# Attention probabilities times the value columns alone, in two column groups, with the softmax sums added on GpSimd and finished by a product with ones

## The chip, the cores and the metric

The kernel runs on one NeuronCore of a Trainium2 chip. The metric is the device time in microseconds (us) of one execution. Before the change it was measured three times: 1147.48 us in the median, from 1145.49 to 1149.68.

## What is computed

Two layers of a diffusion trunk over 256 context tokens and 512 latent tokens, model width 1024, all in float32. Each layer projects the normalised tokens, runs three mixers side by side (gated linear attention "GLA", six heads of latent attention "MLA", six query heads of grouped attention "GQA" on two key/value heads), gates them and multiplies by an output matrix. The change is in the softmax attention of the twelve MLA and GQA heads:

```python
def attend(q, keys, vals, scale):
    s = jnp.einsum('bqhgd,bkhd->bhgqk', q, keys) * scale
    p = jax.nn.softmax(s.astype(jnp.float32), axis=-1).astype(vals.dtype)
    return jnp.einsum('bhgqk,bkhe->bqhge', p, vals)
# latent queries (512) attend to context and latent keys (768); context queries (256) to context keys
y = latent_attention(q, k, v, kc, vc, scale) * silu(z)
yc = attend(qc, kc, vc, scale) * silu(zc) if l < DEPTH - 1 else None
```

Value vectors have 64 columns in both kinds of heads. Layer 1 needs no context outputs.

## The kernel before, in words

Five engine programs are written by hand and meet through semaphores: `up(stage, step)` marks a step as done, `at(stage, step)` is the value another engine waits for. Each engine works strictly in the order in which its program is written. SP issues all weight blocks `W`, two buffers in turn, when TensorE has finished the block before last. Of PSUM's eight banks six form a ring: `open_` (L1238) takes the next one for each group of products and waits until the group six places before was released with `let_go`; the two `pv` banks hold the attention outputs, in turn.

**Scores and exponentials.** Scores are made transposed, a tile of 128 keys by all queries of a block, so that the exponential needs no transpose before it meets the values. A head is one block of 512 latent queries over six key tiles, and in layer 0 a block of 256 context queries over two key tiles before it. The "units" of a head are these tiles: j = 0 to 7 in layer 0, 0 to 5 in layer 1. The negated maximum of each query is found first (`maxes` L1444 on TensorE, `maxima` L1110 on VectorE, `max_rows` L1460 on TensorE, `neg_max` L741 on ScalarE) and comes in as an extra row of the queries against a row of ones of the keys (97 rows), so ScalarE's one instruction, L771, makes exp(score - max) from PSUM into one of four buffers `prob`. MLA scores are one float32 product (L1548), GQA scores two products of rounded parts (L1552, L1554).

**Values and sums.** `pv` (L1482) multiplies a probability tile by a stationary operand of 128 columns: 64 columns of values and 64 of ones, which lie beside one another in `vm` (MLA, 192 columns for a pair of heads: values, ones, values) and `vg` (GQA, the same shape). For even heads it takes columns 0 to 127, for odd ones 64 to 191. So one half of the `pv` bank gets the unnormalised output and the other half 64 equal copies of the softmax sum. A float32 product is recorded as two matmul records of the same shape. `recip` (L705, ScalarE: Ln, L712, and Exp with scale -1, L714) turns the sums into reciprocals `rd`, and `normalise` (L1136, VectorE: L1145, L1150) multiplies the output by them and by the gate in `Y`.

**The order around it on TensorE** (L1522 to L1569). For each head h: project the queries of head h+1 (`project_q`, L1425), one pending value product, the max rows of head h (L1466), project the keys of h+1 (`project_k`, L1435), the other pending value product; then for each unit the scores, the value products of all but the last two units (`flush(2)`), and from unit `MAX_FROM` on (3 in layer 0, 2 in layer 1) two maximum products of head h+1 (L1457). The projections exist for MLA heads alone, so at the boundaries into heads 5 to 11 only value products and max rows stand. In layer 0 heads 1 to 4, and heads 7 and 8 of both layers, also carry a modulation block: `mod` (L1273) multiplies eight tiles of weights in four column groups of 32, and `mod_turn` (L1284, L1290) turns the rows. The GLA output (`gla_o`, L1394) writes two 64-column products into the two halves of a bank (L1399).

**GpSimd** (L366 to L492): rounds the keys of each MLA head (`round_k`, L384), fills `vm`'s ones (L437), fills the padding rows of the GQA keys and queries (`k_pad`, L459 and L460; `q_pad`, L464, which `maxes` of heads 6 and up wait for), subtracts the rounded output weights from the weights (`w_lo`, L471, sixteen instructions a layer, needed by the out products L1579 to L1581), issues the DMAs that bring the residual back (`x_back`, L478 and L482). It makes the block masks of GLA's states too (L430).

**ScalarE** (L756 to L811) has for each head: copies of the next head's queries and keys (`head_in`, `gqa_in`), the exponentials, `recip` of the head before behind exponential 0 and of the context block behind exponential 3, `round_q`, in the last two heads sixteen `w_high` roundings (L733), and at the end of the layer `y_high` (L738).

## Time and profile before

| | |
|---|---|
| three timed runs, median (range) | 1147.48 us (1145.49 to 1149.68) |
| profiled execution, first to last instruction | 1146.1 us |
| mean granted TensorE clock | 0.974 of full |
| TensorE matmul busy | 1072.0 us, 94% |
| weight loads | 610.6 us, 53% |
| VectorE, ScalarE, GpSimd busy | 440.2, 368.3, 127.5 us |
| instructions | 11426 |
| layer 0 attention, MLA and GQA heads | 362 to 584 us of the span |
| layer 1 attention | 945 to 1088 us |

The profiled execution's own time is known as its span, 1146.1 us; the device time that is measured without a profile has its median 1.4 us above it. A busy share counts an engine's instructions, not its waits. Matmul records overlap in a stream, since a record's length holds the array's latency: a 512-wide float32 record is 0.59 us long while the next one starts 0.43 us behind it. The chain of waits, which follows the work that ended last, therefore counts such a record with 0.43 us. Granted clock 1.00 is 2.4 GHz, 0.5 is 1.2 GHz.

### The profile page before, as it was taken

The page shows a single profiled execution, that of the slowest core. Times are in us where ns is not written, and L with a number is a line of the kernel's source. Part 1 is how long each engine was busy: PE and PEld are TensorE (multiplying, and loading weights), DVE is VectorE, ACT ScalarE, POOL GpSimd, SP SyncE. Part 2 cuts the span into 40 slices and gives each one's busy share as a digit, 9 for nine tenths or more (in the row PEclk, how much of TensorE's full clock was granted, in tenths as well). Part 3 has the DMA queues.
Part 4 walks back from the last instruction along what each step waited for, and adds up shares of the span by engine and source line. Part 5 has one row for each costly group of instructions (what it writes and reads, how often), then busy time and mean ns, then how long its engine had stood idle before and what let it go on. Part 6 is the DMA issues. An engine that isn't in the chain of part 4 may idle for free.

```text
span 1146.1 us, 11426 instructions
## 1 busy us (share of the span) xinstructions
PE 1072.0 (94%) x4139; PEld 610.6 (53%) x4139; DVE 440.2 (38%) x797; ACT 368.3 (32%) x690; POOL 127.5 (11%) x148
## 2 busy tenths in 40 slices
PE   2799999999999999999899899999998999999996
PEld 0455555655455544455568655555444544445474
DVE  1342103312473433554453433122237444454453
ACT  3322113100113344566650332112001234455712
POOL 2000000000242001000440200000003300100530
PEclk8899999999999999999999899999998899999998
DMA  9801012201200222122022411120222000003021
GB/s 351 288 1 56 2 54 74 74 19 56 74 1 1 74 74 77 71 74 74 1 111 69 145 51 55 55 73 1 74 75 73 1 1 1 0 29 119 1 93 73
DMA packets 50965, 74.29 MB, mean 65 GB/s; under 512 B 7812, under 2 KB 30688, under 8 KB 50784
## 3 DMA queue, kind: packets, MB, share of 16 engines
q1 hardware_dynamic: 47088, 60.81, 15.8%
q0 software_dynamic: 3824, 12.77, 3.0%
q8 instruction: 35, 0.57, 0.2%
q14 instruction: 18, 0.15, 0.0%
HBM read 69.37 MB, written 4.19 MB: 64 GB/s over the span
## 4 chain that ended last, share of the span: by engine, by line
PE 86%; DVE 4%; issue 3%; ACT 3%; DMA 2%; POOL 1%; SPq 1%; ACTq 0%; POOLq 0%; DVEq 0%
PE bank L1329 30%; PE pv L1497 10%; PE bank L1548 6%; PE bank L1320 5%; PE bank L1457 3%; PE bank L1579 3%; PE bank L1581 3%; PE bank L1580 3%; PE bank L1435 3%; PE bank L1466 3%; PE bank L1425 2%; DMA W<-in_w_mod 2%; PE bank L1273 2%; PE bank L1405 2%; PE bank L1474 2%
## 5 line engine op out<-in xcount | busy, mean ns | idle before, releaser
L1329 PE MATMUL bank<-hA,W 128*128 128x512 f32 (+1 forms) x992 | 348.3, 510 | 2.7 <-DVE hA L882 1.5
L1329 PEld LDWEIGHTS bank<-hA,W 128*128 128x128 f32 x992 | 187.8, 190 | 154.3 <-issue 142.4
L771 ACT ACTIVATE hA<-bank 128x512 f32<-128x512 f32 (+1 forms) x168 | 93.1, 563 | 91.9 <-PE bank L1548 64.0
L1127 DVE TENSOR_REDUCE mxp<-bank 128x1 f32<-128x384 f32 x192 | 96.5, 551 | 51.0 <-PE bank L1457 50.8
L1497 PE MATMUL pv<-hA,vg 128*128 128x512 f32 (+1 forms) x168 | 85.1, 588 | 6.7 <-ACT hA L771 6.4
L1497 PE MATMUL pv<-hA,XA 128*128 128x512 f32 (+1 forms) x168 | 82.1, 570 | 1.5 <-ACT hA L771 1.5
L1548 PE MATMUL bank<-hA 97*128 97x512 f32 (+1 forms) x168 | 78.1, 565 | 0.0
L1145 DVE SCALAR_TENSOR_TENSOR hA<-pv,hA 64x512 f32<-64x512 f32 (+1 forms) x36 | 21.6, 600 | 113.5 <-ACT hA L714 113.3
L1320 PE MATMUL bank<-W,hA 128*128 128x384 f32 x192 | 63.7, 486 | 0.0
L1580 PE MATMUL bank<-W_parts,hA_parts 128*128 128x512 f32 x160 | 62.3, 389 | 0.0
L911 DVE SCALAR_TENSOR_TENSOR YA<-tz,bank 128x512 f32<-128x512 f32 (+1 forms) x24 | 14.4, 599 | 108.3 <-ACT tz L573 108.3
L573 ACT ACTIVATE tz<-bank 128x512 f32<-128x512 f32 (+1 forms) x24 | 12.6, 527 | 134.1 <-PE bank L1329 134.1
L412 POOL MEMSET hA<- 128x2048 f32 x2 | 3.6, 1807 | 447.1 <-PE bank L1329 447.1
L1497 PEld LDWEIGHTS pv<-hA,XA 128*128 128x128 f32 x168 | 30.3, 189 | 40.4 <-issue 37.3
L1320 PEld LDWEIGHTS bank<-W,hA 128*128 128x128 f32 x192 | 36.5, 190 | 26.5 <-issue 3.8
L1457 PE MATMUL bank<-rounded 96*128 96x384 f32 (+1 forms) x108 | 45.3, 505 | 2.6 <-DVE nmx L1119 1.6
L536 ACT ACTIVATE tz<-XA 128x1024 f32<-128x1024 f32 x16 | 16.9, 1054 | 91.3 <-DVE XA L1229 88.8
L520 ACT ACTIVATE rs<-bank,eps 128x512 f32<-128x512 f32 (+1 forms) x20 | 12.0, 602 | 96.2 <-PE bank L1348 57.6
L1497 PEld LDWEIGHTS pv<-hA,vg 128*128 128x128 f32 x168 | 29.0, 191 | 25.5 <-ACT hA L771 12.7
L1224 DVE TENSOR_TENSOR rt<-bank,cqkv 128x512 f32<-128x512 f32 x20 | 13.8, 692 | 67.4 <-PE bank L1581 53.6
L1548 PEld LDWEIGHTS bank<-hA 97*128 97x128 f32 x168 | 30.4, 189 | 16.3 <-issue 15.0
L1273 PE MATMUL bank<-W,sc 128*32 128x512 f32 x192 | 29.3, 738 | 9.6 <-DMA W<-in_w_mod 8.7
(209 smaller groups left out, 1467.9 us busy)
## 6 DMA issues: line engine op xcount, KB each, us to landing
W<-in_w_mod SPq DMA_DIRECT2D x12, 2048.0 KB, 8.0
W<-in_w_in SPq DMA_DIRECT2D x6, 1536.0 KB, 8.5
W<-in_w_in SPq DMA_DIRECT2D x8, 1024.0 KB, 6.1
W<-in_w_out SPq DMA_DIRECT2D x4, 2048.0 KB, 7.8
W<-in_w_in SPq DMA_DIRECT2D x8, 512.0 KB, 4.3
XA<-in_x SPq DMA_DIRECT2D x4, 512.0 KB, 10.9
XA<-in_x POOLq DMA_DIRECT2D x4, 512.0 KB, 7.4
x_between_layers<-XA POOLq DMA_DIRECT2D x4, 512.0 KB, 2.9
```

Of the source, the lines that this page charges most:

```text
L771: act.activation(prob[slot % 4][:, 0:nq], ps("sc", l, h, q0, kt)[:, 0:nq], ACT.Exp, scale=MLA_SCALE if h < MLA_H else GQA_SCALE)\
L1127: dve.tensor_reduce(mxp[:, t, half:half + 1], ps("mx", l, h, q0, t, half)[:, 0:384], AX, ALU.max).then_inc(*up("part_max", l, h, q0, t, half))
L1273: mm = pe.matmul(p[32 * j:32 * j + 32, :], sc[:, k, :], W[:, i % 2, k, :], start=(r == 0), stop=(r == 1), skip_group_check=True)
L1320: mm = pe.matmul(p[:, 0:384], hT[:, k, t * P:(t + 1) * P], w[:, k, 0:384], start=(k == 0), stop=(k == KD - 1))
L1329: mm = pe.matmul(p[:, 0:c[1]], w[:, k, s * P:s * P + P], hT[:, k, c[0]:sum(c)], start=(k == 0), stop=(k == KD - 1))
L1435: mm = pe.matmul(p[0:64, 0:c[1]], wukv[:, f, h, 0:64], cqkv[:, 2 + f, c[0]:sum(c)], start=(f == 0), stop=(f == 1))
L1457: close(pe.matmul(p[:, 0:n], q[:, t * P:t * P + P], k[:, n * half:n * half + n], start=True, stop=True), "mx", l, h, q0, t, half)
L1466: mm = pe.matmul(p[96:97, P * j:P * j + P], nmx[:, h % 2, t:t + 1], ident, start=True, stop=True)
L1497: mm = pe.matmul(pv_banks[i % 2][:, 0:nq], v, prob[sl % 4][:, 0:nq], start=(kt == 0), stop=(kt == nkt - 1))
L1548: mm = pe.matmul(p[:, 0:nq], kh[h % 2][0:97, keys], qh[h % 2][0:97, queries], start=True, stop=True)
L1579: pe.matmul(p[:], hi, w_hi[n][k], start=(k == 0), stop=False)
L1580: pe.matmul(p[:], hi, w_lo[:, i % 2, k, :], start=False, stop=False)
```

## The change

The value tiles lose their ones: `vm` and `vg` hold 64 columns for each head. Each value product becomes two, with the same 64 value columns stationary: the first half of the queries goes to partitions 0 to 63 of the `pv` bank, the second half to partitions 64 to 127. The sums are made elsewhere: GpSimd adds a block's probability tiles as they come (`prob_sums`, one add a tile from the second on) into one of two buffers `psum`, and TensorE multiplies that total by 64 columns of ones, in the same two halves (`den`), behind the scores of unit 0 of the next head (latent block) or behind unit 3 (context block). `den` takes a bank of the ring. ScalarE's reciprocal reads that bank: 128 partitions by half the queries. `normalise` scales in two instructions. The probability buffers are six instead of four, and the exponential waits for the buffer's add as well as its product. On GpSimd the whole order of the attention part is rewritten into one loop over heads.

```diff
+PROBS = 6
-        prob = [hA[:, 3072 + 512 * i:3584 + 512 * i] for i in range(4)]
-        rd, un = hA[:, 5120:5632], hA[:, 5632:6144]
+        rd, un = hA[:, 5120:5376], hA[:, 5632:6144]
-        vm = XA[:, 0:3456].rearrange("p (t r c) -> p t r c", t=TILES, r=3)
+        vm = XA[:, 0:2304].rearrange("p (t h v) -> p t h v", t=TILES, h=MLA_H)
-        vg = sb("vg", [P, TILES, 2, 192])
+        vg = sb("vg", [P, TILES, 2, 64])
+        more = sb("more", [P, 4, 512])
+        prob = [hA[:, 3072 + 512 * i:3584 + 512 * i] for i in range(4)] + [more[:, i, :] for i in range(2)]
+        psum = [more[:, 2 + i, :] for i in range(2)]
...
GpSimd:
-                pool.memset(vm[:, :, :, 64:128], 1.0).then_inc(*up("vm_ones", l))
...
-                for h in heads[1:MLA_H]:
-                    round_k(l, h)
...
+                def prob_sums(h, q0, nq, nk):
+                    i = pv_index(l, h, q0)
+                    total = psum[i % 2][:, 0:nq]
+                    first = slot_of(l, h, q0)
+                    if i >= 2:
+                        pool.wait_ge(*at("filled", "den", *pv_owner(i - 2)))
+                    pool.wait_ge(*at("prob", l, first + 1))
+                    pool.tensor_tensor(total, prob[first % PROBS][:, 0:nq], prob[(first + 1) % PROBS][:, 0:nq],
+                                       ALU.add).then_inc(*up("prob_sum", l, first + 1))
+                    for sl in range(first + 2, first + nk // P):
+                        pool.wait_ge(*at("prob", l, sl))
+                        pool.wait_ge(*at("prob_sum", l, sl - 1))
+                        pool.tensor_tensor(total, total, prob[sl % PROBS][:, 0:nq], ALU.add)\
+                            .then_inc(*up("prob_sum", l, sl))
+                    pool.wait_ge(*at("prob_sum", l, first + nk // P - 1))
...
+                for h in heads:
+                    if len(qbs(l)) == 2:
+                        prob_sums(h, *qbs(l)[0])
+                    if h + 1 < MLA_H:
+                        round_k(l, h + 1)
+                    if h == MLA_H - 1:
...
+                            pool.memset(k_low[g][64:96, :].bitcast(F32), 0.0).then_inc(*up("k_pad", l, g, 0))
+                            pool.memset(k_low[g][96:97, :].bitcast(F32), 1.0).then_inc(*up("k_pad", l, g, 1))
+                    if h in (MLA_H - 1, MLA_H):
+                        b = h - MLA_H + 1
+                        pool.wait_ge(*at("filled", "sc", l, MLA_H + b - 2, 256, TILES - 1))
+                        pool.wait_ge(*at("k_pad", l, 1, 1))
+                        pool.memset(q_high[b][64:96, :].bitcast(F32), 0.0).then_inc(*up("q_pad", l, b))
+                    if h == MLA_H + 1:
...
+                                pool.dma_start(X[:, t, :], src).then_inc(*dma("x_back", l))
...
+                    prob_sums(h, *qbs(l)[-1])
+                    if h == heads[-2]:
+                        weights_low(0, range(4))
...
+                weights_low(0, range(4, KD))
+                weights_low(1, range(KD))
...
ScalarE, recip:
+                    n2 = nq // 2
+                    act.wait_ge(*at("filled", "den", l, h, q0))
+                    act.activation(rd[:, 0:n2], ps("den", l, h, q0)[:, 0:n2], ACT.Ln).then_inc(*up("den_ln", l, h, q0))
+                    let_go(("den", l, h, q0), "den_ln", l, h, q0)
+                    act.activation(rd[:, 0:n2], rd[:, 0:n2], ACT.Exp, scale=-1.0).then_inc(*up("recip", l, h, q0))
...
ScalarE, exponentials:
-                        if slot >= 4:
-                            act.wait_ge(*at(*prob_reader(l, slot - 4)))
+                        if slot >= PROBS:
+                            act.wait_ge(*at(*prob_reader(l, slot - PROBS)))
+                            act.wait_ge(*at("prob_sum", l, summed(l, slot - PROBS)))
...
VectorE, normalise:
+                    for e in range(2):
+                        half = slice(64 * e, 64 * e + 64)
+                        dve.scalar_tensor_tensor(out=un[r:r + 64, n2 * e:n2 * e + n2], in0=pv[half, 0:n2], scalar=0.5,
+                                                 in1=rd[half, 0:n2], op0=ALU.mult, op1=ALU.mult)\
+                            .then_inc(*up("o_scaled", l, h, q0))
...
TensorE:
-                    mm = pe.matmul(pv_banks[i % 2][:, 0:nq], v, prob[sl % 4][:, 0:nq], start=(kt == 0),
-                                   stop=(kt == nkt - 1))
+                    v = vm[:, kt, h, :] if h < MLA_H else vg[:, kt, (h - MLA_H) // 3, :]
+                    for e in range(2):
+                        mm = pe.matmul(pv_banks[i % 2][64 * e:64 * e + 64, 0:n2], v,
+                                       prob[sl % PROBS][:, n2 * e:n2 * e + n2], start=(kt == 0), stop=(kt == nkt - 1))
...
+                def den(h, q0, nq, nk):
+                    p, n2 = open_("den", l, h, q0), nq // 2
+                    total = psum[pv_index(l, h, q0) % 2]
+                    pe.wait_ge(*at("prob_sum", l, slot_of(l, h, q0) + nk // P - 1))
+                    for e in range(2):
+                        mm = pe.matmul(p[64 * e:64 * e + 64, 0:n2], ones[:, 0:64], total[:, n2 * e:n2 * e + n2],
+                                       start=True, stop=True)
+                    close(mm, "den", l, h, q0)
...
                         flush(2)
+                        if j == 0 and h:
+                            den(h - 1, *qbs(l)[-1])
+                        if j == 3 and len(qbs(l)) == 2:
+                            den(h, *qbs(l)[0])
                         if j >= MAX_FROM[l]:
                             maxes(groups[:2])
...
                 flush(0)
+                den(heads[-1], *qbs(l)[-1])
```

The copies of values become one instruction a tile on VectorE (`mla_v`, and the GQA part of "tok") instead of two.

## Rows read from the trace of the kernel before

**Rows 1.** The page, part 1: busy time and share of the span of each engine.
```profile
PE 1072.0 (94%) x4139; PEld 610.6 (53%) x4139; DVE 440.2 (38%) x797; ACT 368.3 (32%) x690; POOL 127.5 (11%) x148
```

**Rows 2.** Windows: window, length, busy us (instructions), TensorE's clock, DMA.
```profile
490.00:584.00 94.00, 85.33 (x341) 48.62 (x340) 48.23 (x90) 64.01 (x119) 21.34 (x17) 0.98 0.13 45
```

**Rows 3.** Chain of waits in layer 1's MLA heads: start us, us, what.
```profile
954.60 0.35 PE bank L1457 x2
954.95 0.86 PE bank L1548 x2
955.81 0.86 PE pv L1497 x2
...
962.63 2.73 PE bank L1435 x8
965.36 1.05 PE pv L1497 x2
```

**Rows 4.** Groups of TensorE by shape: count, busy us, mean ns, idle before.
```profile
L1497 PE MATMUL pv<-hA,vg 128*128 128x512 f32 x144 | 77.2, 618 | 3.3 <-ACT hA L771 3.0
...
L1497 PE MATMUL pv<-hA,vg 128*128 128x256 f32 x24 | 7.9, 409 | 3.5 <-ACT hA L771 3.4
```

**Rows 5.** Timeline of TensorE, layer 0, head 6: start us, us, what [idle before].
```profile
493.22 0.70 PE L1497 MATMUL pv<-hA,vg 128*128 128x256 f32 x2 [1.18 <-ACT hA L771]
```

**Rows 6.** Timeline of TensorE, layer 1, a boundary between GQA heads.
```profile
1064.10 1.03 PE L1466 MATMUL bank<-con,nmx 128*1 128x128 f32 x8 [0.27 <-DVE nmx L1131]
```

**Rows 7.** Timeline of TensorE, the GLA output of layer 0.
```profile
341.95 0.65 PE L1399 MATMUL bank<-hA,XA 128*64 128x256 f32 x4 [0.43 <-POOL hA L430]
342.53 0.82 PE L1405 MATMUL bank<-glav,hA 128*128 128x64 f32 x3
```

**Rows 8.** Chain of waits around a modulation block of layer 0.
```profile
384.39 1.85 PE bank L1273 x16
386.24 1.06 PE bank L1548 x2
```

**Rows 9.** Groups of ScalarE by shape: the reciprocal's two instructions.
```profile
L714 ACT ACTIVATE hA<-hA 64x512 f32<-64x512 f32 x24 | 15.1, 629 | 0.8
L712 ACT ACTIVATE hA<-pv 64x512 f32<-64x512 f32 x24 | 14.2, 592 | 0.7
...
L714 ACT ACTIVATE hA<-hA 64x256 f32<-64x256 f32 x12 | 5.0, 415 | 0.4
...
L712 ACT ACTIVATE hA<-pv 64x256 f32<-64x256 f32 x12 | 4.5, 379 | 0.3
```

**Rows 10.** Two lines of GpSimd: count, duration ns min/median/max.
```profile
L430 POOL TENSOR_TENSOR hA<-XA,con x20: 1028/1170/1515, 306.6 to 893.0; 128x512 f32<-128x512 f32 x20
...
L471 POOL TENSOR_TENSOR W_parts<-W,gqk_parts x12: 1255/1270/1450, 559.6 to 1077.9; 128x512 fp32r<-128x512 f32 x12
...
L471 POOL TENSOR_TENSOR W_parts<-W,sq_parts x4: 1482/1738/1987, 580.5 to 1094.0; 128x512 fp32r<-128x512 f32 x4
```

**Rows 11.** Timelines, layer 0, heads 4 and 5: GpSimd, ScalarE, TensorE.
```profile
454.44 0.73 POOL L459 MEMSET wuq_parts<- 32x768 f32 x1
...
456.80 0.73 POOL L460 MEMSET wukv_parts<- 1x768 f32 x1
...
476.52 0.38 ACT L771 ACTIVATE hA<-bank 128x256 f32<-128x256 f32 x1
...
477.37 0.59 PE L1457 MATMUL bank<-wuq_parts,hA_parts 96*128 96x256 f32 x2
```

**Rows 12.** Timeline of TensorE in head 10 of layer 0; the window behind it.
```profile
562.84 0.74 PE L1457 MATMUL bank<-wukv_parts,hA_parts 96*128 96x384 f32 x2 [2.10 <-DVE nmx L1119]
...
563.00:567.00 4.00, 4.00 (x11) 2.67 (x11) 2.90 (x7) 2.93 (x6) 4.00 (x4) 0.69 0.02 4
```

**Rows 13.** Timelines at the end of layer 0's attention: ScalarE, TensorE.
```profile
582.13 1.06 ACT L771 ACTIVATE hA<-bank 128x512 f32<-128x512 f32 x2
...
584.17 0.80 PE L1579 MATMUL bank<-gqk_parts,hA_parts 128*128 128x512 f32 x1
```

More of the change, by code:

```diff
@@ L304, in pv_owner, with slot_of, summed @@
             return (0, i // 2, (0, 256)[i % 2]) if i < 24 else (1, i - 24, 256)
+        def slot_of(l, h, q0):
+            return h * sum(nk // P for _, _, nk in qbs(l)) + (2 if q0 and l < DEPTH - 1 else 0)
+        def summed(l, slot):
+            per = sum(nk // P for _, _, nk in qbs(l))
+            u = slot % per
+            return slot + 1 if u == 0 or (l < DEPTH - 1 and u == 2) else slot
         def prob_reader(l, slot):
@@ L370, in _ @@
             pool.memset(keep[:], 1.0).then_inc(*up("pool_init", "keep1"))
-            pool.memset(vg[:, :, :, 64:128], 1.0).then_inc(*up("pool_init"))
             pool.memset(wa[:], 0.0).then_inc(*up("pool_init", "wa"))
@@ L450, in _, with weights_low @@
                             .then_inc(*dma("brow_in", l))
[L451 to L467 removed]
+                def prob_sums(h, q0, nq, nk):
[13 more added lines that the diff above has]
+                    pool.wait_ge(*at("prob_sum", l, first + nk // P - 1))
+                def weights_low(n, ks):
                     i = W_POS[("out", l, n)]
[L469 removed]
+                    for k in ks:
                         pool.wait_ge(*at("w_hi", l, n, k))
@@ L920, in _ @@
                             src = ps("tok", l, t)[:, 256:384].rearrange("p (g v) -> p g v", g=2)
-                            for half in range(2):
-                                dve.tensor_copy(vg[:, t, :, 128 * half:128 * half + 64], src)\
-                                    .then_inc(*up("vg", l, t, half))
-                            let_go(("tok", l, t), "vg", l, t, 1)
+                            dve.tensor_copy(vg[:, t, :, :], src).then_inc(*up("vg", l, t))
+                            let_go(("tok", l, t), "vg", l, t)
                     elif item == "ga":
```

77 lines of the change are left out of this document (29 added, 48 removed).

## The prediction

> **What bounds the kernel now.** I read the page's busy shares, then the stages in a table of windows, then the chain of waits inside the attention stages, and last the timelines of single heads. The page: TensorE is busy for 94% of the span, VectorE for 38%, ScalarE for 32%, GpSimd for 11% [rows 1]. The window of layer 0's GQA heads, where TensorE is least full in attention: 85.3 of 94 us, with GpSimd at 21.3, nearly all of it w_lo's subtractions in the last two heads [rows 2]. The chain of layer 1's MLA heads shows TensorE alone: one key tile of a head is 0.35 us of maximum products, 0.86 us of scores and 0.86 us of probabilities times values [rows 3]. The last term is what the change halves on paper. All 512-wide value products are 144 (two records each, half of them on the GQA values' tile, half on the MLA values') and the 256-wide ones 24 [rows 4].
>
> So TensorE's time is the time, except in three places, which decide here. At the start of GQA heads, and in the last two heads of a layer, TensorE waits for ScalarE's exponentials: 1.18 us in head 6 [rows 5]. At a boundary without projections (into heads 5 to 11) the max rows wait for VectorE's last maximum, 0.27 us after TensorE is ready [rows 6].
>
> **A value product in two column groups.** Today: 0.86 us [rows 3]. After: two products of 256 columns, side by side. The same shape runs already in the GLA output, L1399: four records (two products of 128x64 by 128x256) start together at 341.95, and the next full-width weights load at 342.53, 0.58 us later; in a row they would stream 0.86 us [rows 7]. So they do overlap. Of the 0.58, 0.43 is streaming (half of 0.86) and 0.15 is entry and drain. The full-width instruction behind a tiled stretch pays again: eight modulation products in four groups take 1.85 us, 0.13 over two rounds of 0.86, and the scores behind them take 1.06 instead of 0.86 [rows 8]; the key projection, 64 columns, takes 2.73 us where its 512- and 256-wide products stream 2 x 0.86 + 2 x 0.43 = 2.58, and the value product behind it 1.05 [rows 3]. A tiled stretch between full-width work thus costs about 0.35 us beyond its streaming (0.13 to 0.15 going in, 0.20 coming out). An isolated pair costs 0.43 + 0.35 = 0.78, and gains **0.08 us**, not 0.43. The ends are 0.58 (a gain of 0.28, if nothing is paid behind it) and 0.86 + 0.35 = 1.21 (no overlap; [rows 7] speak against it); I take 0.78, which two other lines confirm.
>
> The Trainium skill (TensorEngine Tiling (Array Packing), Theoretical Speedup) gives a stationary operand of at most 64 columns up to twice the speed, and its Key Properties say that changing the tiling mode drains TensorE. By the first alone the gain of a pair would be 0.43 us; the trace has the overlap and also the drain, in the 0.20 us of [rows 8].
>
> **The sum on TensorE's path.**
> - Latent products between scores and maxima: 4 in each head, in the 20 heads that aren't ScalarE-bound: 80 x 0.08 = **-6.4**.
> - Products at head boundaries. Into heads 1 to 4 the first stands before the max rows (tiled already, so one switch is saved: 0.86 + 0.15 - 0.43 - 0.30 = 0.28) and the second behind the key projection (no switch in: 0.43). 8 x 0.71 = **-5.7**. Into heads 5 to 11 the first one's gain goes into VectorE's maximum, the second one's mostly into the row copy and ScalarE; I leave **-0.9**.
> - Sums of a latent block: a pair of the same shape behind scores 0 of the next head, 0.78. Thirteen are on TensorE's path (into heads 1 to 4 of layer 0; into 1 to 4 and 6 to 10 of layer 1), 10.1 less 1.2 of slack where TensorE waits for ScalarE now; the other nine hide in such waits (if that cover goes, 0.78 each). **+8.9**.
> - Context blocks (layer 0): pairs are 128 wide, 0.21 + 0.35 against 0.43, **+0.13**; the second has the sums pair beside it (two pairs in one stretch, 0.43 + 0.35 + 0.04), **+0.39**. Five MLA heads: **+2.6**. In GQA heads 6 to 9 that sums pair also waits for GpSimd's add of the second exponential and holds up what is behind it on TensorE, about 0.5 each: **+2.0**.
> - ScalarE's reciprocal is 128x256 instead of 64x512: at the 0.38 and 0.42 that the 256-wide forms take, against 0.59 and 0.63 [rows 9], 0.42 less. It counts where ScalarE is last: nine heads, and 0.2 for the context block in two: **-4.2**.
>
> **What moves on GpSimd.** 120 adds of 128x512 and 12 half as wide. The nearest rows: 1.03 to 1.52 us for L430, 1.27 and 1.74 for L471's groups (the second beside VectorE's SBUF work) [rows 10]. I take 1.27. A key tile takes TensorE 1.6 us (GQA) to 2.0 us (MLA), so the adds keep up; hidden behind TensorE, and at 1.74 not quite (a rival).
>
> The order is the trouble. Head 5's k_pad and q_pad memsets were run during head 4, right behind the last rounding of keys (four from 454.44 on, 0.79 apart; q_pad's follow at the same length [rows 11]). Now in layer 0 they stand behind the context add of head 5, which waits for head 5's second exponential, over at 476.52 + 0.38 = 476.9 [rows 11], or 0.42 earlier with the shorter reciprocal. Then 0.6 (add) + 5 x 0.79 gives 481.0, and the maxima of head 6, which need q_pad, start now at 477.37 [rows 11]: TensorE stands for **+3.7 us**, with all that is queued behind it. In head 6 one memset stands there the same way: **+0.6**. In layer 1 there is no context block and the memsets fall due before head 5 starts: nothing. The x_back DMA issues move before head 7's latent adds (six issues of about half a us, and the adds behind them catch up within the six probability buffers), nothing; the SP queue is untouched.
>
> The clock. An idle time of 2.10 us before L1457 at 562.84 is followed by a window at a granted clock of 0.69, that is, partly at 1.2 GHz instead of 2.4 [rows 12]. A stand of 3.7 us I expect to do the same; at the lower level some 3.4 us of work cost 1.7 more: **+1.7**.
>
> The ends of the layers. The last sums pair waits for the last add. In layer 0 the last two exponentials run from 582.13 for 1.06 us, the out products start at 584.17 [rows 13]; the last add ends some 1.3 us behind its exponential, and its pair (0.78) stands before them: **+1.9**, and 0.9 in layer 1, where VectorE's y_lo covers part. w_lo's late subtractions (12 x 1.27 to 1.74 = 15 to 21 us) are needed from 10 us on, k by k, and for the second half after more than 21: nothing.
>
> VectorE: normalise is two instructions instead of one, beside fewer copies of values: nothing, since it is busy for 51% of that window [rows 2]; if not, 0.2 a head.
>
> Sum: -6.4 - 5.7 - 0.9 + 8.9 + 2.6 + 2.0 - 4.2 + 3.7 + 0.6 + 1.7 + 2.8 = **+5.1 us**. On the profiled span of 1146.1 that is 1151.2; the median is 1.4 us above that span, so **1152.5 us**.
>
> **Rivals.**
> - *Switches hide, faster.* Place: the next full-width load behind each pair. If it is prefetched, a pair costs 0.58, and 93 pairs on TensorE's path (80 and 13) gain 0.20 more: -18.6, **1134**. For it: the next load starts at 0.58 [rows 7]. Against: the 0.20 stands behind both 64- and 32-column work [rows 3, 8]. It decides from about 0.12 us a pair. With no switch cost at all (the skill's doubling, same section) 93 x 0.35 = 33: 1120. Together 0.12, of which 0.03 for the second.
> - *The waits are absorbed, no change.* The memsets' stand and the drop of the clock (5.4 us) don't reach the end, since ScalarE and VectorE work ahead meanwhile and TensorE's head 5 was waiting anyway: **1147**. Against: maxima and scores are in one queue. 0.25.
> - *GpSimd binds, slower.* Adds at 1.74 exceed a GQA key tile's 1.6, lag grows by 0.7 us a head and shows at the sums pairs of twelve GQA heads: +8.4, **1161**. For it: L471's slow group; against: VectorE mostly reads PSUM here. 0.15. The skill (GPSIMD Engine Reference, Engine selection) advises against elementwise work with two inputs on GpSimd, as about twice as slow as VectorE; the price here is the 1.27 to 1.74 above.
> - *The change doesn't do what it says:* the two products don't overlap, 93 x 0.43 = +40, **1192**. Two lines show overlap [rows 7, 8]: 0.03.
> - My forecast: 0.42. Something else: 0.03.
>
> **How the numbers follow.** A measurement of this kernel can tell about 0.3%, 3.4 us, from no change. Faster: the first rival, and a fifth of the second with the rest, 0.20. Same (1144.1 to 1150.9): most of the second, and the forecast's own low side, 0.25. Slower: 0.55. The range takes in the second and third rival and the forecast, and, of the first, the cases down to a pair at 0.66 us (93 x 0.12 = 11 less): 1141 to 1165; the forecast's own is 1149 to 1157.
>
> **What would show it.** A steady MLA tile 0.08 us shorter, with the instruction behind each pair 0.2 longer than now [rows 3]; in layer 0 a wait of 3 to 4 us of L1457 at head 5 for a GpSimd memset, and a lower clock behind it; adds at 1.2 to 1.4 us; sums pairs without waits except at the layers' ends. I am wrong if the pair costs under 0.6 (then 1134 to 1140), or the maxima of head 6 don't wait, or adds pass 1.6 us.

## The result and the profile after

The changed kernel took **1176.46 us** (median of 4 runs, 1170.23 to 1180.07) against 1147.59 for the kernel before beside it: a ratio of 1.025, with an interval of 1.022 to 1.028. The forecast was 1152.5, slower, with a range up to 1165. The sign was right; 28.9 us more where 5.1 had been summed up, and outside the range. The profiled execution took 1177.12 us, its span is 1175.3.

The page of the kernel after, part 1 (busy us, share, instructions of each engine), against [rows 1]:
```profile
PE 1085.0 (92%) x4619; PEld 590.5 (50%) x4619; DVE 472.6 (40%) x809; ACT 353.6 (30%) x690; POOL 299.8 (26%) x277
```
TensorE's busy time rose by 13 us, though each value product streams half as long. VectorE's rose by 32 us, with almost the same instructions.

The steady state of layer 1's MLA heads, in the chain of waits (start us, us, what; line numbers are those of the kernel after: L1498 maxima, L1597 scores, L1536 value pairs, L1549 the ones products), against [rows 3]:
```profile
971.72 0.58 PE pv L1536 x4
972.30 0.55 PE bank L1498 x2
972.85 0.86 PE bank L1597 x2
...
985.24 1.06 PE bank L1597 x2
986.30 0.58 PE bank L1549 x4
```
A key tile is 0.58 + 0.55 + 0.86 = 1.99 us against 2.07: the two products overlap, and what stands behind them (here the maxima) takes 0.20 more than its 0.35. The gain of a pair is the 0.08 us that was forecast.

Where the 29.2 us between the two profiled spans are, measured between the starts of the max rows of each head and of the out products (after minus before):

| stretch | us |
|---|---|
| start of the program up to head 0 | -0.3 |
| layer 0: heads 0 to 4 | -0.1 |
| **layer 0: head 5** | **+10.8** |
| **layer 0: head 6** | **+4.7** |
| layer 0: heads 7 to 10 | +1.9 |
| layer 0: head 11, up to the out products | +3.7 |
| out products of layer 0 and layer 1's projections | +0.2 |
| layer 1: heads 0 to 5 | -2.7 |
| **layer 1: GQA heads 6 to 11** | **+12.7** |
| end | -1.8 |

So the MLA heads won what the pairs give, and three places lost ten times that. The first is head 5 of layer 0. Timelines of GpSimd and TensorE there, and windows (window, length, busy us of PE, PEld, DVE, ACT, POOL with instructions, TensorE's clock, DMA):
```profile
475.99 0.98 POOL L470 TENSOR_TENSOR more<-more 128x256 f32<-128x256 f32 x1 [7.01 <-ACT more L815]
477.03 0.73 POOL L497 MEMSET wuq_parts<- 32x768 f32 x1
...
480.27 0.73 POOL L504 MEMSET hA_parts<- 32x768 f32 x1
```
```profile
481.25 0.79 PE L1498 MATMUL bank<-wuq_parts,hA_parts 96*128 96x256 f32 x2 [3.70 <-POOL hA_parts L504]
```
```profile
480.00:500.00 20.00, 18.75 (x49) 7.67 (x50) 5.00 (x11) 2.76 (x5) 7.18 (x7) 0.50 0.00 1
...
507.00:514.00 7.00, 7.00 (x22) 3.58 (x23) 6.18 (x10) 1.20 (x3) 3.42 (x3) 0.52 0.00 0
```
The stand (TensorE waits with everything behind it in its queue) is there, for the instruction that was named, and as long as forecast (3.7 us). Behind it TensorE ran for 20 us at a granted clock of 0.50, that is, at 1.2 GHz, though it was busy for 94% of that stretch; the forecast had allowed for one short window.

The second place is head 6 of layer 1. VectorE's timeline in front of the maxima, and what TensorE waited for:
```profile
1034.63 1.64 DVE L1137 CAST wukv_parts<-gqk 64x768 fp32r<-64x768 f32 x1
1036.30 1.91 DVE L1139 TENSOR_TENSOR wukv_parts<-gqk,rounded 64x768 fp32r<-64x768 f32 x1
1038.24 1.64 DVE L1145 TENSOR_TENSOR hA_parts<-gqk,rounded 64x512 fp32r<-64x512 f32 x1
1039.91 2.88 DVE L1166 TENSOR_REDUCE mxp<-bank 128x1 f32<-128x384 f32 x6
```
```profile
1040.62 1.12 PE L1498 MATMUL bank<-wuq_parts,hA_parts 96*128 96x384 f32 x2 [3.61 <-DVE mxp L1166]
```
In the kernel before these three take 0.55, 0.95 and 0.69 us. Now each shares its time with a GpSimd add, and the maxima, which read PSUM and keep their 0.55 us apiece, start 3 us later. TensorE stands for 3.61 us in front of the next maximum products, until one of these maxima is done.

The waits of TensorE in attention (line waited in, line that released it: us in total, times, longest), and GpSimd's groups against [rows 10]:
```profile
PE bank L1498 <- DVE mxp L1166: 6.4, 4, 3.6
PE bank L1507 <- DVE nmx L1170: 6.1, 11, 0.6
PE bank L1549 <- POOL more L475: 5.2, 2, 3.2
PE bank L1498 <- POOL hA_parts L504: 4.5, 2, 3.7
...
PE bank L1601 <- DVE cumA L1202: 3.7, 2, 1.9
```
```profile
L475 POOL TENSOR_TENSOR more<-more,hA 128x512 f32<-128x512 f32 x56 | 74.1, 1324 | 31.5 <-ACT hA L815 27.8
...
L483 POOL TENSOR_TENSOR W_parts<-W,rounded 128x512 fp32r<-128x512 f32 x6 | 11.1, 1868 | 0.0
```
The adds take 1.32 us on average, as costed. L1549 <- L475 is the last sums pair at the two layers' ends (3.2 and 2.0 us). L1601 <- L1202, the scores of heads 7 and 8 behind VectorE's gate bias, was in no step of the forecast.

### The profile page after: what moved, and what is told of

Same layout as the page of the kernel before. It is cut to its first block, busy times and chain, and to the rows that moved or that the text cites. A ratio compares the mean times of both kernels' runs of the same rounds, so it can differ in the third digit from the quotient of the medians.

```text
span 1175.3 us, 12700 instructions
## 1 busy us (share of the span) xinstructions
PE 1085.0 (92%) x4619; PEld 590.5 (50%) x4619; DVE 472.6 (40%) x809; ACT 353.6 (30%) x690; POOL 299.8 (26%) x277
## 4 chain that ended last, share of the span: by engine, by line
PE 84%; POOL 3%; DVE 3%; issue 3%; ACT 3%; DMA 2%; SPq 1%; ACTq 0%; POOLq 0%; DVEq 0%
PE bank L1370 30%; PE bank L1597 6%; PE pv L1536 6%; PE bank L1361 5%; PE bank L1498 5%; PE bank L1633 3%; PE bank L1634 3%; PE bank L1635 3%; PE bank L1476 3%; PE bank L1507 3%; PE bank L1466 2%; PE bank L1446 2%; PE bank L1314 2%; PE bank L1515 1%; PE bank L1601 1%
## 5 line engine op out<-in xcount | busy, mean ns | idle before, releaser
L1597 PE MATMUL bank<-hA 97*128 97x512 f32 (+1 forms) x168 | 86.0, 604 | 0.1
L475 POOL TENSOR_TENSOR more<-more,hA 128x512 f32<-128x512 f32 x56 | 74.1, 1324 | 31.5 <-ACT hA L815 27.8
L815 ACT ACTIVATE hA<-bank 128x512 f32<-128x512 f32 (+1 forms) x112 | 62.1, 560 | 65.6 <-PE bank L1597 43.7
L1186 DVE SCALAR_TENSOR_TENSOR hA<-pv,hA 64x256 f32<-64x256 f32 (+1 forms) x72 | 27.2, 378 | 105.1 <-ACT hA L758 103.7
L470 POOL TENSOR_TENSOR more<-hA 128x512 f32<-128x512 f32 (+1 forms) x28 | 35.5, 1266 | 117.7 <-ACT hA L815 100.0
L475 POOL TENSOR_TENSOR more<-more 128x512 f32<-128x512 f32 x40 | 52.3, 1308 | 26.8 <-ACT more L815 25.0
L815 ACT ACTIVATE more<-bank 128x512 f32<-128x512 f32 (+1 forms) x56 | 31.4, 564 | 56.2 <-PE bank L1597 34.2
L1536 PE MATMUL pv<-hA,vg 128*64 128x256 f32 (+1 forms) x224 | 37.7, 417 | 1.0 <-ACT hA L815 1.0
L1536 PE MATMUL pv<-hA,XA 128*64 128x256 f32 (+1 forms) x224 | 38.5, 407 | 0.0
L1597 PEld LDWEIGHTS bank<-hA 97*128 97x128 f32 x168 | 29.4, 196 | 17.4 <-issue 16.0
```

The source lines that it names most:

```text
L470: pool.tensor_tensor(total, prob[first % PROBS][:, 0:nq], prob[(first + 1) % PROBS][:, 0:nq], ALU.add).then_inc(*up("prob_sum", l, first + 1))
L475: pool.tensor_tensor(total, total, prob[sl % PROBS][:, 0:nq], ALU.add)\
L815: act.activation(prob[slot % PROBS][:, 0:nq], ps("sc", l, h, q0, kt)[:, 0:nq], ACT.Exp, scale=MLA_SCALE if h < MLA_H else GQA_SCALE)\
L1536: mm = pe.matmul(pv_banks[i % 2][64 * e:64 * e + 64, 0:n2], v, prob[sl % PROBS][:, n2 * e:n2 * e + n2], start=(kt == 0), stop=(kt == nkt - 1))
L1597: mm = pe.matmul(p[:, 0:nq], kh[h % 2][0:97, keys], qh[h % 2][0:97, queries], start=True, stop=True)
```

## The experiments

Each kernel ran beside the kernel before, whose medians were 1147.1 to 1148.8 us. A step of a head is given as its difference to the kernel before, from one profiled execution. In kernels with the same code in a head these steps agree to 0.1 or 0.2 us, unless the clock fell in one of them; the start of the program differs by up to 8 us between executions and is left out of such sums. The lower level of the clock is 1.2 GHz. The length of one low stretch is read from the clock's record in the trace of one execution; the time at the lower level in a whole execution is 2 x (1 - mean clock) x span, and the mean clock is known for every run. Work at the lower level takes at most twice as long, so a us there costs at most half a us.

### The stand and the clock

**late_pads**, the kernel before with one wait ahead of the k_pad memsets:
```diff
                 pool.wait_ge(*at("round_k", l, MLA_H - 1))
+                if l == 0:
+                    pool.wait_ge(*at("prob", l, 8 * (MLA_H - 1) + 1))
                 for g in range(2):
```


> The kernel before the change with one wait more: in layer 0 GpSimd's k_pad and q_pad memsets wait for the second exponential of head 5's context block. Nothing else differs, no pairs and no adds. Theory A (stand, then clock): a wait of the first maxima in head 5 of 3 to 4 us, a low clock behind it, and 8 to 12 us in all: 1156 to 1160. Rival B (the stand costs itself and one short window): 3.7 + 1.7 = 5.4 us, 1153. Rival C (the clock falls only with the pairs): 1151.

Measured: 1154.90 us, ratio 1.005 (1.003 to 1.007), 6.9 us above the kernel before, between A and B; head 5 +6.5; the other heads within 0.1, save head 10 of layer 0 (-1.6: the short low window that the kernel before has there [rows 12] is missing).

**pairs_late**, the same wait in pairs_only (below), so with the value pairs in two column groups and without adds.

> pairs_only (no adds; softmax sums left out of the computation) with the one wait of late_pads: layer 0's k_pad and q_pad memsets wait for head 5's second context exponential. It tells why the same stand of 3.7 us cost 6.5 us without pairs and 10.8 us in the kernel after. Theory A (with the value pairs in the mix the clock, once down, stays down longer): head 5 costs 9 to 12 us over pairs_only and the low window behind it is 10 us or more; 1159 to 1163. Rival B (the rest of the 10.8 is the adds'): 6 to 7 us, one window of up to 7 us, 1157.

Measured: 1158.16 us, ratio 1.010 (1.008 to 1.012), 7.3 above pairs_only; head 5 +10.2, which is 10.9 over pairs_only. TensorE's stand in the two timelines, late_pads and pairs_late:
```profile
483.04 0.79 PE L1459 MATMUL bank<-wuq_parts,hA_parts 96*128 96x256 f32 x2 [3.58 <-POOL hA_parts L466]
```
```profile
481.57 0.78 PE L1487 MATMUL bank<-wuq_parts,hA_parts 96*128 96x256 f32 x2 [4.04 <-POOL hA_parts L510]
```
and two windows behind it in each, in the same order:
```profile
482.00:488.00 6.00, 4.96 (x9) 2.92 (x10) 1.42 (x4) 0.60 (x1) 0.73 (x1) 0.50 0.00 0
...
492.00:502.00 10.00, 8.50 (x38) 4.83 (x36) 3.73 (x8) 5.68 (x10) 0.73 (x1) 1.00 0.01 2
```
```profile
482.00:488.00 6.00, 6.00 (x14) 2.23 (x15) 1.78 (x4) 0.80 (x2) 0.00 (x0) 0.50 0.01 3
...
492.00:502.00 10.00, 10.00 (x38) 4.20 (x34) 2.21 (x5) 2.15 (x5) 0.73 (x1) 0.54 0.00 0
```
In these two executions the same stand is followed by one low stretch of 6.8 us with 128-column value products, and by one of 20.5 us with 64-column pairs, as in the kernel after. The stand and its clock cost 6.5 and 10.9 us there. So 10.8 us in head 5 need no adds; that much pairs_late shows.

That the pairs make the low stretch longer, theory A's point, is not shown. Over all executions the stand costs the same with and without them: 6.9 us in late_pads, 7.3 in pairs_late, which is rival B's figure. The profiled execution of late_pads had a mean clock of 0.977, but six of its ten had 0.970 to 0.973, 9 to 16 us more at the lower level; all four of pairs_late had 0.963 to 0.969. By the medians the stand adds 17 us at the lower level without pairs (0.979 to 0.9715) and 20 with them (0.973 to 0.9645).

**pads_early**, the kernel after with the memsets moved: the block of k_pad to `h == MLA_H - 2`, that of q_pad one head earlier and behind the latent adds:
```diff
-                    if h == MLA_H - 1:
+                    if h == MLA_H - 2:
                         pool.wait_ge(*at("filled", "kp", l, MLA_H - 1, LAT))
...
                     prob_sums(h, *qbs(l)[-1])
+                    if h in (MLA_H - 2, MLA_H - 1):
+                        b = h - MLA_H + 2
...
+                        pool.memset(q_high[b][64:96, :].bitcast(F32), 0.0).then_inc(*up("q_pad", l, b))
```


> The kernel after the change, with head 5's k_pad memsets behind the last rounding of keys (in head 4) and each q_pad memset behind the latent adds of the head before, so that none stands behind the context add of head 5. Theory A (the order on GpSimd costs a stand of TensorE, and the stand costs the clock): layer 0's heads 5 and 6 lose their 10.8 + 4.7 = 15.5 us over the kernel before, and the time falls from 1176.5 to 1161 (1158 to 1165); no window at 0.50 between 480 and 513 us. Rival B (the low clock comes from the tiled pairs, not from the stand): only the 3.7 + 0.8 us of waits go, 1172, and a low clock stays in that stretch.

Measured: 1168.08 us, ratio 1.018 (1.014 to 1.021), 8.4 below the kernel after, between A and B. Head 5 fell from +10.8 to +0.6 as theory A has it; but heads 6 and 7 kept +4.1 and +2.3. There VectorE's slowed operations stood in front of the maxima as in layer 1 (its 64x768 subtraction took 1.92 us), TensorE waited 1.70 us, and a new low stretch of 10.2 us followed. The memsets were one cause of two in this stretch, and with the first away the second showed.

### TensorE's part alone

**pairs_only**: pads_early without GpSimd's adds; the ones products read a constant tile (the softmax sums are left out of the computation).
```diff
                 def prob_sums(h, q0, nq, nk):
+                    return
...
-                            act.wait_ge(*at("prob_sum", l, summed(l, slot - PROBS)))
...
-                    pe.wait_ge(*at("prob_sum", l, slot_of(l, h, q0) + nk // P - 1))
+                    pe.wait_ge(*at("pool_init", "psum"))
```

> The kernel after the change with the memsets in the same early order and without GpSimd's adds: the ones products read a constant tile, so the softmax sums (and with them the output) are left out of the computation. TensorE's work is that of the kernel after. Theory A (the pairs and the ones products are priced about right, and the loss is on GpSimd and the clock): 1142 to 1146, from -6.4 - 5.7 - 0.9 + 8.9 + 2.6 - 4.2 = -5.7 us against the kernel before. Rival B (the switches of tiling cost more than 0.35 us a stretch): above 1150.

Measured: 1150.85 us, ratio 1.002 (1.000 to 1.004). Layer 1's MLA heads -0.3 to -0.6 each, the GQA heads between -0.5 and +0.1, save heads 7 and 8 with +1.5 each, which no term had. By the time alone that is B's bound, 5 us above A's window; but the MLA heads' steps speak against B, since they gain and a dearer switch would show in each of them. The clock tells more: the mean granted clock is 0.973 (median of 10 runs) where the kernel before has 0.979 (19 runs). That is 62 us at the lower level against 48, an estimate of at most 7 us of the pairs' gain that went back into the clock. What lowers it is open: adds_only (below), without a single pair, has 0.970.

### The adds

**adds_only**: the kernel before with the adds of pads_early beside it (in all heads but the last of each layer) and its order on GpSimd, their sum in a tile that nothing reads, five probability buffers, and an exponential that waits for the add of its buffer.

> The kernel before the change with GpSimd's adds of the probability tiles beside it (heads 0 to 10 of each layer, five probability buffers, the sum in an unused tile that nothing reads), memsets in the early order; TensorE's and VectorE's work as before. Theory A (GpSimd's adds slow VectorE's work in SBUF, which is last in the GQA heads): about 10 to 14 us slower than before, 1158 to 1161, nearly all of it in heads 6 to 11 of layer 1, VectorE's 64x512 subtraction and product at 1.2 to 1.4 us instead of 0.69. Rival B (VectorE is late in the kernel after for another reason, such as the ring of banks behind the tiled pairs): within 3 us of before.

Measured: 1165.84 us, ratio 1.016 (1.013 to 1.019), above A's 1161. Layer 1's heads 6, 9, 10: +3.4, +2.0, +3.3; heads 7, 8, 11: 0. Layer 0, where A expected next to nothing, paid too: heads 5 and 6 +1.6 and +3.6, its out products +3.0. There w_lo's subtractions, now later, stand beside VectorE's y_lo (the outputs less their rounded part): four of these take 7.79 us instead of 4.94, and TensorE waits 2.0 us for them.

**adds_low_first**: adds_only with the change of order on VectorE of low_first (below).

> adds_only (the kernel before with GpSimd's adds beside it, the sum unused), and VectorE's low parts of the GQA queries ahead of the normalisation. Theory A (the price of the adds is VectorE's doubled operations ahead of the maxima): most of layer 1's +3.4, +2.0 and +3.3 in heads 6, 9 and 10 and of layer 0's +1.6 and +3.6 in heads 5 and 6 goes; 1166 less 8 to 11, 1155 to 1158. Rival B (ScalarE held up by GpSimd's release of the probability buffers, or total work): within 4 us of 1166.

Measured: 1153.38 us, ratio 1.004 (1.002 to 1.006), 12.5 below adds_only, more than expected. The same instructions in adds_only,
```profile
1026.83 1.93 DVE L1147 TENSOR_TENSOR wukv_parts<-gqk,rounded 64x768 fp32r<-64x768 f32 x1
1028.79 1.64 DVE L1153 TENSOR_TENSOR hA_parts<-gqk,rounded 64x512 fp32r<-64x512 f32 x1
1030.46 1.95 DVE L1174 TENSOR_REDUCE mxp<-bank 128x1 f32<-128x384 f32 x4
```
and in adds_low_first:
```profile
1014.09 0.69 DVE L1157 TENSOR_TENSOR hA_parts<-gqk,rounded 64x512 fp32r<-64x512 f32 x1
...
1015.29 0.95 DVE L1146 TENSOR_TENSOR wukv_parts<-gqk,rounded 64x768 fp32r<-64x768 f32 x1
```
There they lie between the adds of two heads. So 121 adds on an engine that was idle for 89% of the time cost 18 us, and two thirds of it was VectorE's low parts standing in the wrong place (12.5 us by the medians; the two profiles show 10.1 of it behind the start of the program). The Trainium skill (SBUF - State Buffer, "SBUF: two separate sides") says that VectorE and GpSimd share a pair of SBUF ports, which VectorE needs where its instruction has two inputs from SBUF or runs in a two-port mode, and that whichever starts first holds it for its whole instruction while the other waits. The rows agree: 1.64 less 0.69 is within one add, and the reductions, which read PSUM, don't change.

### VectorE's order

**low_first**, on pads_early; low_queries is the part of low_parts at L1145, low_keys the one at L1137 and L1139:
```diff
                 for h in heads:
+                    if MLA_H <= h + 1 < len(heads):
+                        low_queries(h + 1)
+                        if h + 1 > MLA_H:
+                            low_keys(h + 1)
                     if h:
                         normalise(h - 1, *qbs(l)[-1][:2])
...
-                    if MLA_H <= h + 1 < len(heads):
-                        low_parts(h + 1)
+                    if h + 1 == MLA_H:
+                        low_keys(h + 1)
```


> The memsets in the early order, and VectorE's low parts of the GQA queries (and of the second pair's keys) ahead of the normalisation of the head before instead of behind it, in a stretch where VectorE waits 4 to 6 us for ScalarE's reciprocal. Theory A (GpSimd's adds double VectorE's SBUF operations, and those stand ahead of the maxima): taken out of that chain they cost little, layer 1's heads 6 to 11 fall from +12.7 to about +3 us over the kernel before and layer 0's heads 6 and 7 from +6.4 to +2, so 1168 less 11 to 14: 1154 to 1157. Rival B (VectorE is late by its total work, wherever it stands): 1164 to 1168.

Measured: 1155.88 us, ratio 1.008 (1.005 to 1.010), 12.2 below pads_early: theory A. Head 6 of layer 1 went from +3.9 to -1.4, heads 9 and 10 to -0.2 and +0.1; heads 7 and 8 stand at +3.9 and +2.3 (before: +2.5 and +2.3). In this profile head 5 of layer 0 cost +6.0 with no long wait in it: the clock stood at the lower level for 17 us from 479.5 on. In low_last, with the same code there, it didn't fall (+0.1).

**before_order**: the kernel before with the order of low_first and of gate_first.

> The kernel before the change with VectorE's order of mended_den as far as it applies: the low parts of the queries and the gate bias ahead of the normalisation. Theory A (the order mends what the change broke; the kernel before has VectorE early enough): within 2 us of the kernel before. Rival B (the order is worth the same there): 4 us or more faster.

Measured: 1146.08 us, ratio 0.998 (0.996 to 0.999), 2.7 us less. That is nearer to A than to B, though the interval (0.9 to 4.7 us) takes in both bounds; 2.1 of the 2.7 us that layer 0's heads gain in the profile are head 10's, where the low window of [rows 12] is missing. The order is worth 12 us only where the adds are.

**gate_first**, on low_twos_last (below):
```diff
+                    m = mod_of_head(l, h)
+                    if m and m[2] >= 4:
+                        gate_bias(*m[1:])
                     if h:
                         normalise(h - 1, *qbs(l)[-1][:2])
-                    m = mod_of_head(l, h)
-                    if m:
-                        (mod_cols if m[2] < 4 else gate_bias)(*m[1:])
+                    if m and m[2] < 4:
+                        mod_cols(*m[1:])
```


> low_twos_last with VectorE's gate bias (heads 7 and 8) ahead of the normalisation instead of behind it. Theory A (the normalisation now comes later, since its reciprocal waits for the ones products behind scores 0; the gate bias waits behind it, keeps the modulation's bank, and TensorE's scores stand for that bank, 2.7 us each): layer 1's heads 7 and 8 fall from +5.3 and +3.9 to about +0.5 over the kernel before, layer 0's from +2.7 to +0.5: 1147 less 5 to 9, 1138 to 1142. Rival B (the ring is full for another reason): 1145 to 1148.

Measured: 1138.80 us, ratio 0.992 (0.991 to 0.994), 8.0 below low_twos_last: theory A. Layer 1's heads 7 and 8: -0.6, -0.5. The wait that went, in low_twos_last:
```profile
1048.07 0.80 PE L1612 MATMUL bank<-hA_parts,wuq_parts 128*128 128x512 f32 x1 [2.65 <-DVE cumA L1206]
```
The normalisation used to wait for the last value product of the head before; now it waits for the ones products behind scores 0 and the reciprocal behind them. The gate bias stood behind it in VectorE's queue and held the modulation's bank, and the scores stood for that bank. It is also most of the +1.5 of pairs_only, where TensorE waits 1.1 us for the gate bias in each of the two heads. In layer 0 head 7 kept +2.7; mended took it.

### Fewer tiled stretches, and the layers' ends

**low_twos**, on low_first; two key tiles' pairs stand together behind every second scores product:
```diff
-                        flush(2)
+                        if j % 2:
+                            flush(2)
```

> low_first, and the value pairs issued in twos: two key tiles' pairs in one tiled stretch behind every second scores product, so 36 (layer 0) and 24 (layer 1) tiled stretches fewer with the same products. Theory A (a tiled stretch costs 0.35 us beyond its streaming, 0.15 going in and 0.20 coming out): 60 x 0.35 = 21 us on paper, less where ScalarE or VectorE is last: 12 to 18 below low_first, and the steady MLA heads of layer 1 shorter by 2 x 0.35 = 0.7 us each. Rival B (the pairs' cost is elsewhere, or the exponentials and the ring of banks bind once pairs are late): within 4 us of low_first, MLA heads unchanged.

Measured: 1150.82 us, ratio 1.002 (1.000 to 1.004), 5.1 below low_first. Two key tiles in layer 1's chain:
```profile
948.09 0.86 PE bank L1604 x2
948.95 1.01 PE pv L1543 x8
949.96 0.55 PE bank L1505 x2
950.51 0.86 PE bank L1604 x2
951.37 0.36 PE bank L1505 x2
```
These are 3.64 us, against 2 x 1.99 singly: a stretch costs 0.34 beyond its streaming, as costed (0.35). The MLA heads gain 0.7 to 1.0 us each, save the two heads 5, in one of which low_first has a low stretch and in the other low_twos. But the time gained a third of A's figure. The median clock is 0.9645: 82 us at the lower level against 65 in low_first, by estimate at most 8 us of what was won. Theory A is right in its price, and wrong in the sum, which took the clock as given.

**low_last**, on low_first: in the last head of each layer the adds stop two key tiles short, and `den` runs three ones pairs, on the last two probability tiles and on the sum.
```diff
+                    used = nk // P - (2 if h == heads[-1] and q0 else 0)
-                    for sl in range(first + 2, first + nk // P):
+                    for sl in range(first + 2, first + used):
```

> low_first, and in the last head of each layer GpSimd adds only the first four key tiles; the ones products take the last two probability tiles directly (three pairs in one stretch). Theory A (the wait of the last sums pair is GpSimd's lag): the waits of 3.2 and 2.0 us at the layers' ends go, for 2 x 0.9 us more of ones products: 3 to 4 us below low_first. Rival B (y_hi and y_lo of the last head are late anyway, from the same exponentials): within 1 us of it.

Measured: 1154.69 us, ratio 1.006 (1.004 to 1.009), 1.2 below low_first and within its spread, so the medians don't tell. The profile does: head 11 goes from +3.1 to +0.6 in layer 0 and from +1.6 to -0.4 in layer 1. But the stretches behind it give 0.7 and 1.6 us of that back, so about 2 us are left, between A and B. What stood there in the kernel after (TensorE, GpSimd):
```profile
603.89 1.12 PE L1549 MATMUL bank<-more,ones 128*64 128x256 f32 x4 [3.17 <-POOL more L475]
```
```profile
600.02 3.73 POOL L475 TENSOR_TENSOR more<-more 128x512 f32<-128x512 f32 x2
```
**low_twos_last**: all of these.

> Early memsets, low parts first, pairs in twos and the short last sum together. If the three parts add up: 1154 to 1157 less 12 to 18 less 3, so 1134 to 1142, faster than the kernel before. If the pairs in twos don't pay: 1150 to 1154, slower than it.

Measured: 1146.77 us, ratio 0.999 (0.997 to 1.002). Short of the window; the clock (0.969) and heads 7 and 8 (+5.3, +3.9, mended in gate_first) hold the rest.

**mended**: gate_first, and for a context block `den` takes `rest = [end - 2, end - 1]`, the probability tiles themselves, with no add on GpSimd.

> gate_first, and layer 0's context sums taken by the ones products from the two probability tiles directly (0.2 us more of TensorE in each of 12 heads, no add and no wait for one). Theory A: the waits for GpSimd's 256-wide adds (2.8 us in 5 places) go for 12 x 0.2: within 1.5 us of gate_first, 1137 to 1142. Rival B (GpSimd's 12 adds of 0.75 to 1.0 us crowd VectorE as well): 3 us or more below gate_first.

Measured: 1131.56 us, ratio 0.987 (0.985 to 0.988), 7.2 below gate_first: rival B. The heads that gained are layer 0's 7 (from +2.7 to -0.5) and 5 (-0.6 to -1.4); nothing but the context adds and their waits had changed. Head 7 in gate_first, GpSimd, VectorE and TensorE:
```profile
504.21 2.08 POOL L507 DMA_DIRECT2D XA<-in_x  x4
506.31 1.28 POOL L470 TENSOR_TENSOR more<-more 128x512 f32<-128x512 f32 x1
```
```profile
505.65 2.23 DVE L1195 TENSOR_TENSOR YA<-hA,YA 64x256 f32<-64x256 f32 x1
```
```profile
508.48 0.41 PE L1508 MATMUL bank<-wuq_parts,hA_parts 96*128 96x384 f32 x1 [1.55 <-DVE nmx L1162]
```
and the same VectorE product in mended:
```profile
503.74 0.42 DVE L1202 TENSOR_TENSOR YA<-hA,YA 64x256 f32<-64x256 f32 x1
```
The context add had pushed GpSimd's x_back issues back, and with them the first latent add (506.31), to where VectorE multiplies in front of the maxima; in mended the issues are over at 498.1. The product took 2.23 us instead of 0.42 and ended 0.3 us behind that add; TensorE waited 1.55 us behind it, and a low stretch of 3.4 us followed, which mended doesn't have. Layer 0's heads together explain 3.2 us of the 7.2, and head 5 of layer 1 lost 1.5 (a low stretch of 3.4 us stands in it). What the rest is stays open; the mean clock (0.9735 against 0.971) can hold at most 3 us of it by estimate.

**mended_den**: mended, and in layer 1 the ones products of a head and its reciprocal stand beside two value pairs of the next, the normalisation behind the maxima.
```diff
-                        if j == 0 and h:
+                        if j == (0 if l == 0 else 3) and h:
                             den(h - 1, *qbs(l)[-1])
```

> mended, and in layer 1 the ones products of a head stand behind the first two value pairs of the next head (one tiled stretch instead of two), the reciprocal and the normalisation behind them. Theory A (0.35 us a stretch): 11 x 0.35 = 3.9 us below mended less what ScalarE hides, 2 to 4 us. Rival B (the later normalisation makes something else late): 0 or slower.

Measured: **1126.30 us, ratio 0.983** (0.981 to 0.984), 5.3 below mended, more than A's 2 to 4. The MLA heads of layer 1 are at -1.3 to -2.1. Heads 1 to 4 gained 0.3 to 0.4 each, A's price of a stretch; head 5 gained 3.0, in part because mended's low stretch is missing there, heads 9 and 10 1.3 and 1.0, and heads 7 and 8 lost 0.9 each.

**mended_single**: mended_den with the pairs singly again.

> mended_den with the value pairs singly behind each scores product again, as the change has them. Theory A (a tiled stretch costs 0.35 us, and low_twos gained 0.7 to 1.0 us a head by it): about 15 us slower than mended_den, 1139 to 1144, still a little faster than the kernel before; the pairs singly are worth no more than 1%. Rival B (the gain of mended_den is mostly the order): within 6 us of 1126.

Measured: 1143.95 us, ratio 0.996 (0.994 to 0.998), 17.7 above mended_den: theory A, a little over its 15 (the profiles show 13.6 behind the start of the program). With the waits of the adds mended, the change as it was meant is worth 0.4%, of which the order alone gives 0.2% in before_order; that the pairs stand together makes it 1.7%.

## Why the prediction was wrong

**Right.** The isolated pair at 0.78 (0.58 and 0.20 behind it) and its gain of 0.08; the stretch's 0.35; the MLA heads, if anything better than priced (-2.7 in layer 1, where the terms give about -1.6: 24 x -0.08, 4 x -0.71 and 4 x 0.78). The stand of TensorE in head 5: place, cause and 3.7 us. The adds at 1.27 (1.32 measured), which bound only at the layers' ends and, for 2.1 us in three places, at context blocks. The sign, in part by luck: TensorE's own part (the terms in the expectation of pairs_only) was summed up as a gain of 5.7 us, and pairs_only measured 2.8 us more time, not less.

**Wrong, in four steps.**
- *"At the lower level some 3.4 us of work cost 1.7 more: +1.7."* The term was sized too small, after one short low window [rows 12]. The low stretch was 20.5 us long and a second one of 6.8 followed in head 6. In the profiled executions the clock's part is 2.9 us in late_pads (6.5 less 3.6) and about 7 in pairs_late (10.9 less 4.0). In head 5 alone this is 5.4 of the 24 us that were missing.
- *"VectorE: nothing, since it is busy for 51% of that window [rows 2]."* This is the largest of the four. The mean share hid that three SBUF operations stand in a row in front of the maxima, for which TensorE waits. adds_only and adds_low_first price it at 12.5 us. The sign was in [rows 10]: L471 at 1.74 beside VectorE's work in SBUF. That row was read as a price for GpSimd alone; in the kernel after both were slowed, the add from 1.27 to 1.87 us and the subtraction from 0.69 to 1.64. The x_back issues were also put at nothing; in head 7 of layer 0 they push an add onto VectorE's 64x256 product, which takes 1.91 us instead of 0.42. The rival "GpSimd binds" had the right heads and the wrong engine.
- *The gate bias* was not a step at all. The change makes the reciprocal wait for one more product in TensorE's queue, and the prediction did not name what is queued behind the normalisation: 1.5 us a head in pairs_only, more beside the adds. That is 3.0 of the 8.5 us between the -5.7 and the +2.8 of TensorE's own part; the other 5.5 go with the lower clock (at most 7 us) and with what the profile doesn't show, which stays open.
- *The layers' ends* at 1.9 and 0.9. Layer 0's was +3.7: the last two adds took 1.87 us each, beside VectorE and behind four of w_lo's subtractions. Layer 1's was +1.4 up to the out products, but the stretch behind them was 1.8 shorter, so nothing was lost there.

The range failed because three of these were taken at the lower end of what their rows allowed, all together, and the fourth was missing.

## What to carry to other kernels

An idle engine is not a free one. Before work is moved to GpSimd, list the SBUF operations that VectorE runs at the same moment and ask which of them stands in front of something TensorE needs; those go first in VectorE's queue, into a stretch where it waits anyway. A tiled product between full-width ones costs its entry and exit each time, so tiled products are put together. And a stand of TensorE is priced with the clock behind it, as a range: the low stretch behind the same stand was 6.8 us in one execution and 20.5 in another.

## What the runs showed of the hardware

- In two single executions the same stand of 3.6 to 4.0 us was followed by 6.8 us at 1.2 GHz (late_pads, 128-column value products) and by 20.5 us (pairs_late, 64-column pairs), though TensorE was busy for 17.5 of the 20 us from 482 on in the first and for all of them in the second. The medians of all executions don't show that the pairs are what makes it longer.
- Most kernels with pairs have a lower mean clock (0.973 in pairs_only, 0.9645 in low_twos, 0.979 in the kernel before), but adds_only and late_pads, without pairs, have 0.970 and 0.9715 and mended_den, with pairs in twos, has 0.976. The runs of low_first went from 1149.1 to 1163.3 us; its profile has a low stretch of 17 us where that of low_last, with the same code, has none. What sets the clock stays open. The Trainium skill (TensorE: Matmul & The Clock Gate, Part 1) ties the clock to how busy TensorE has been; by busy time alone the stretch that was busy throughout would not be the longer low one, so that does not explain these rows.
- A VectorE operation from SBUF beside a GpSimd add takes up to 1.64 instead of 0.69 us, or 1.91 instead of 0.95, also a plain CAST with one operand (1.64 instead of 0.55), and a 64x256 product 2.23 instead of 0.42, beside the end of GpSimd's DMA issues and an add; one from PSUM keeps its 0.55.
